# One layer's way from the output projection into its experts: projection in column parts, router logits read in place, rank and gather work reordered

## Chip, cores and metric

The kernel runs on one core of a Trainium2 chip. The metric is the device time in microseconds of one execution. All arithmetic is fp32. TensorE multiplies matrices into PSUM banks (eight, each 128 partitions by 512 columns), VectorE and ScalarE read and write banks and SBUF, SyncE issues nearly all DMA, GpSimd issues a few loads and the stores.

## What is computed

Two layers of a hybrid network over 288 tokens: 256 of a prompt and 32 of a running sample. A layer is (cut from the reference):

```python
merged = sigmoid(ga) * (a @ w_br_a) + sigmoid(gb) * (o @ w_br_b)       # attention and recurrence, 1024 wide
x = layernorm(DN_ALPHA * x + merged @ w_out, ln1_g, ln1_b)
moe_out = hier_moe(x, w_rg, w_re, w1, w3, w2)
ple_term = jax.nn.sigmoid(x @ w_ple_gate) * (ple @ w_ple)
x = layernorm(DN_ALPHA * x + moe_out + ple_term, ln2_g, ln2_b)

def hier_moe(...):                                                     # 4 groups of 8 experts, top 2 of the best group
    g_prob = softmax(xt @ w_rg);  g_top, g_idx = top_k(g_prob, 1)
    e_logits = (xt @ w_re).reshape(T, 4, 8)[the group g_idx]
    e_top, e_idx = top_k(softmax(e_logits), 2)
    wts = g_top * e_top / e_top.sum();  eidx = g_idx * 8 + e_idx
    return sum over the two experts of wts * ((silu(x @ w1[e]) * (x @ w3[e])) @ w2[e])
```

An expert has three matrices of 1024 x 512, 6.3 MB together, and there are 32 of them: 201 MB for each layer.

## The kernel before

The tokens are three tiles: 0 and 1 of 128 (the prompt), 2 of 32 (the sample). Each engine has one program, written out by hand, and runs it in order. `Book` numbers every TensorE job (a bank filled once) in the order of the lists `MIX_JOBS` and `expert_jobs`, which also give its bank. `job_done(eng, key)` waits until TensorE has finished that job, `emptied` and `job_read` are the signal and the wait for a bank that has been read, `open_bank` makes TensorE wait for the bank's last reader. `step` makes an engine wait for its own last instruction.

**The mix stage.** The output projection is the jobs `("wo", j, t)`: column half j of token tile t, each of two pieces of four 128-row chunks. Tiles go in the order 2, 0, 1 (`MIX_ORDER`). When a half is done, VectorE adds ALPHA * x and takes statistics (`mixed`), then normalises the tile (`normalize`). For tile 1 the normalisation is in two column halves, and the first one signals `x_half`, so that TensorE may transpose it early. TensorE turns the tile (`turn_mixed`, jobs `t1`), ScalarE and VectorE copy one half each into xT, and TensorE multiplies by the router weights `wr` (`router`, jobs `rt`, 36 columns: 4 group logits, 32 expert logits). VectorE then chooses the two experts of each token in a chain of small operations, each waiting for the one before (`route_tile`). It signals `route_out`.

**Rank and gather.** The experts are worked on in eight quads of four, and each expert has 32 places. `rank(t)` counts with small products, for each token, how many earlier tokens chose the same expert (jobs `rk`). `place_tile` turns that into a 0/1 matrix `sel` of tokens by places, and `gather_first` multiplies x by it, which collects the tokens of quad 0, transposed, in two banks (`XT0`, h = 0 and 1). ScalarE copies the first bank, VectorE the second, into `xeT`.

**Quads.** For each quad TensorE does G (gate projection), U (up projection), hT (transposes of silu(G) * U), Y (down projection) and C (combination of the rows into the tokens' sums); for the next quad it gathers the tokens (`gather`). A G, a U and a Y are each 64 TensorE instructions, in halves h = 0 and 1 over the rows of the weights. In quad 0, the transposes of the weighted choice (`ST0`) stand between G and U and wait for `selw_out`. VectorE makes that from the gate values (the loop at L2428 to L2434, then `weigh`), behind its copy of the second XT0 bank. The per-layer embedding term is the jobs `pl` and `pg` (`plain(j, t)` for column half j of tile t), and it is distributed over the program: (0, 2) while the mix stage routes tile 1, (0, 1) behind U of quad 0, (1, 2) behind its Y, and three more in quads 1 to 3 (`LATE_PLAIN`). `plain_gate` on ScalarE takes the sigmoid and `gated` on VectorE the product.

**Weights.** A piece of weights is 1 MiB (1,048,576 bytes) in an SBUF slot. SyncE issues the pieces of a layer in a fixed order, each when its slot has been read for the last time (`wait_used`). While the mix stage runs, 17 expert pieces find a slot. The next four have slots that G of quad 0 reads, and they come in two halves: `load_blocks` waits for `block_used`, which TensorE signals after two of the four chunks of G's first half, and then for `halves_used`, at the end of that half. Three further pieces wait for the end of that G. Then `load_unit` brings two pieces in one transfer of 2 MiB: six pieces (two units and two single pieces) when U of quad 0 is done, eight when Y of quad 0 is done, eight when G of quad 1 is done, and so on.

```python
if name == "G" and g == 0 and h == 0 and c == 1:
    ins.then_inc(block_used, 1)
```

All matrix products but the transposes are recorded at L1036 (`mm`), transposes at L1086, L1481 and L1570.

Of the kernel before, what the change touches and what calls it, by code (L numbers as in the profile page):

```python
# [180 lines left out]
def gated_tensor_jobs():  # L181
# [16 lines left out]
    for t in range(3):  # L198
        for j in range(len(PARTS[t])):
# [37 lines left out]
def expert_jobs(g):  # L237
# [16 lines left out]
    j += [(("Y", 0), 5), (("Y", 1), 6)] + (plain(1, 2, 1, 2) if g == 0 else []) + combine  # L254
# [52 lines left out]
def last_use(key):  # L307
# [14 lines left out]
    if name == "wo":  # L322
        return (name, key[1], 1)
# [100 lines left out]
def build(nc, x_prompt, x_sample, p_prompt, p_sample, cache_ckv, cache_krope, state_hgrn,  # L424
# [6 lines left out]
    with ctx:  # L431
# [28 lines left out]
        wr = sb("wr", 8 * 36)[:, :].rearrange("p (c n) -> p c n", c=8)  # L460
# [129 lines left out]
        mx = sm[:, 32:48]  # L590
        nb = sm[:, 48:64]
# [357 lines left out]
        def _(pool):  # L949
# [10 lines left out]
            for layer in range(DEPTH):  # L960
# [9 lines left out]
                pool.dma_start(wr[:, :, 0:4], w_router_group[layer].rearrange("(p c) n -> p c n", c=8)).then_inc(rows_in, 16)  # L970
                pool.dma_start(wr[:, :, 4:36], w_router_expert[layer].rearrange("(p c) n -> p c n", c=8)).then_inc(rows_in, 16)
# [49 lines left out]
        def _(pe):  # L1021
# [73 lines left out]
            for layer in range(DEPTH):  # L1095
# [256 lines left out]
                def router(t):  # L1352

                    b = open_bank((layer, "rt", t))
                    for c in range(8):
                        if c % 4 == 0:
                            job_read(pe, (layer, "t1", t, c // 4))
                        ins = mm(b[0:NT[t], 0:36], xT[:, c, T0[t]:T0[t] + NT[t]], wr[:, c, :], c == 0, c == 7)
                    done(ins)
# [36 lines left out]
                def rank(t):  # L1396

                    pe.wait_ge(route_out, 3 * layer + MIX_ORDER.index(t) + 1)
                    b = open_bank((layer, "rk", t))
                    for k, s in enumerate(MIX_ORDER[0:MIX_ORDER.index(t)]):  # L1400
                        mm(b[0:NT[t], 0:32], ones[0:NT[s], 0:NT[t]], route[0:NT[s], s, :], k == 0, False)
                    done(mm(b[0:NT[t], 0:32], tri[0:NT[t], 0:NT[t]], route[0:NT[t], t, :], t == MIX_ORDER[0], True))

                def gather_first(tiles):

                    for h in range(2):
                        key = (layer, "XT0", h)
                        b = open_bank(key) if tiles[0] == MIX_ORDER[0] else bank(key)
                        for t in tiles:
                            for c in range(4):  # L1410
                                k = 4 * h + c
                                ins = mm(b[:, c * P:(c + 1) * P], x[0:NT[t], t, k * P:k * P + P], sel[0:NT[t], t, :],
                                         t == MIX_ORDER[0] and c == 0, t == MIX_ORDER[2])
                        if tiles[-1] == MIX_ORDER[2]:
                            done(ins)
# [20 lines left out]
                gather_first((1,))  # L1436
# [91 lines left out]
                for g in range(QUADS):  # L1528
# [62 lines left out]
                    if g == 0:  # L1591
                        plain(1, 2)
# [28 lines left out]
        def _(act):  # L1621
# [40 lines left out]
            for layer in range(DEPTH):  # L1662
# [255 lines left out]
                plain_gate(0, 2)  # L1918

# [44 lines left out]
                for g in range(QUADS):  # L1964
# [19 lines left out]
                    if g == 0:  # L1984
                        plain_gate(1, 2)
# [26 lines left out]
        def _(dve):  # L2012
# [13 lines left out]
            def normalize(k, t, src, first_half=None, summed=None):  # L2026

                n, at = NT[t], ln_place(k, t)
                dve.bn_aggr(mvs[0:n, 2 * t:2 * t + 2], ln_st[0:n, :]).then_inc(ln_var, 1)
# [53 lines left out]
            for layer in range(DEPTH):  # L2083
# [255 lines left out]

                def route_tile(t):  # L2340
# [266 lines left out]
```

## Time and profile before

| | |
|---|---|
| median of 3 runs | 1529.52 us (1528.48 to 1530.48) |
| span of the profiled execution, first to last instruction | 1528.1 us |
| median less profiled span | 1.4 us |
| TensorE busy | 1285.5 us, 84% |
| VectorE busy | 403.9 us, 26% |
| ScalarE busy | 284.9 us, 19% |
| bytes moved by DMA | 488.78 MB, mean 320 GB/s |
| mean granted TensorE clock | 0.915 of 2.4 GHz |
| chain that ended last | TensorE 61%, DMA 34%, VectorE 3% |

A busy TensorE is not one at its peak, since its matmuls are pipelined and their ends are modelled. Times of single instructions are from this one execution, counted from its first instruction. The two layers follow one another with the same program: what layer 0 does at time t, layer 1 does some 750 us later.

### The profile page before, as it was taken

What the parts mean: (1) busy time and instruction counts of PE and PEld (TensorE: products, weight loads), DVE (VectorE), ACT (ScalarE), POOL (GpSimd) and SP (SyncE); (2) the same over time, 40 slices, a digit from 0 to 9 for tenths busy, and PEclk for the clock granted to TensorE, in tenths of its full rate; (3) what the DMA queues carried; (4) which work ended last, traced back from release to release, by engine and by line L of the source; (5) the groups of instructions that cost most, each with busy time, mean ns of one, the idle gap of its engine ahead of it and who ended that gap; (6) DMA issues with size and microseconds to landing.
All of it is one profiled execution on the core that took longest, in us unless ns stands there. A gap on an engine that the chain in (4) does not pass through costs nothing.

```text
span 1528.1 us, 20304 instructions
## 1 busy us (share of the span) xinstructions
PE 1285.5 (84%) x8528; PEld 723.5 (47%) x8529; DVE 403.9 (26%) x1027; ACT 284.9 (19%) x712; POOL 54.0 (4%) x94
## 2 busy tenths in 40 slices
PE   6999999999788767767799999999997886667655
PEld 4766887554332322322276678766442332223211
DVE  4142633542111101001133446245311111011003
ACT  2342522021001101000044434212111011010001
POOL 1300000000000000000022010000000000000000
PEclk9999999999898878788899999999998988788778
DMA  9503434999999999999972043579999999999994
GB/s 332 164 1 111 173 117 180 396 367 429 429 431 429 431 429 430 430 429 431 376 245 84 15 149 120 179 249 392 382 430 430 429 432 429 431 427 432 430 425 167
DMA packets 78799, 488.78 MB, mean 320 GB/s; under 512 B 7216, under 2 KB 13296, under 8 KB 49648
## 3 DMA queue, kind: packets, MB, share of 16 engines
q1 hardware_dynamic: 74240, 476.47, 75.9%
q0 software_dynamic: 4464, 10.93, 2.4%
q8 instruction: 73, 1.20, 0.3%
q14 instruction: 22, 0.18, 0.0%
HBM read 484.48 MB, written 2.89 MB: 319 GB/s over the span
## 4 chain that ended last, share of the span: by engine, by line
PE 61%; DMA 34%; DVE 3%; issue 1%; SPq 1%; ACT 0%; POOL 0%; DVEq 0%
PE bank L1036 59%; DMA ring<-in_w_e_down 12%; DMA ring<-in_w_e_up 9%; DMA ring<-in_w_e_gate 5%; DMA arena<-in_w_e_gate 4%; DMA arena<-in_w_e_up 4%; PE bank L1086 2%; DMA ring<-in_w_in 1%; DVE arena L2153 0%; SPq L933 0%; DVE arena L2041 0%; DVE x_sb L2050 0%; ACT xT L1642 0%; DVE small L2490 0%; DVE arena L2073 0%
## 5 line engine op out<-in xcount | busy, mean ns | idle before, releaser
L1036 PE MATMUL bank<-arena 128*32 128x512 f32 (+11 forms) x2808 | 572.3, 541 | 174.5 <-DMA ring<-in_w_e_up 71.0
L1036 PE MATMUL bank<-ring,arena 128*32 128x512 f32 (+4 forms) x1360 | 422.1, 650 | 32.3 <-DMA arena<-in_w_e_gate 15.7
L1036 PEld LDWEIGHTS bank<-arena 128*32 128x32 f32 (+6 forms) x2808 | 211.0, 137 | 441.1 <-issue 436.3
L1036 PE MATMUL bank<-ring,xT 128*32 128x128 f32 (+5 forms) x1536 | 237.5, 364 | 1.4 <-ACT xT L1642 1.1
L1036 PE MATMUL bank<-xT,ring 128*128 128x288 f32 x768 | 191.8, 407 | 0.0
L1036 PEld LDWEIGHTS bank<-ring,xT 128*32 128x32 f32 (+1 forms) x1536 | 121.6, 137 | 100.9 <-issue 90.5
L1036 PEld LDWEIGHTS bank<-ring,arena 128*32 128x32 f32 (+1 forms) x1360 | 108.5, 131 | 121.1 <-issue 114.4
L1036 PEld LDWEIGHTS bank<-xT,ring 128*128 128x128 f32 x768 | 143.7, 190 | 37.9
L1036 PE MATMUL bank<-arena,x_sb 128*128 128x128 f32 (+1 forms) x768 | 99.7, 282 | 1.4 <-DVE arena L2373 0.8
L1036 PEld LDWEIGHTS bank<-arena,x_sb 128*128 128x128 f32 (+1 forms) x768 | 90.5, 190 | 19.4 <-issue 12.7
L1036 PE MATMUL bank<-cst,arena 128*32 128x512 f32 x144 | 90.5, 788 | 0.0
L2546 DVE TENSOR_TENSOR arena<-arena,bank 128x512 f32<-128x512 f32 x16 | 11.0, 688 | 238.4 <-PE bank L1036 238.4
L1036 PE MATMUL bank<-arena,ring 128*128 128x288 f32 (+2 forms) x352 | 72.9, 372 | 0.0
L1036 PE MATMUL bank<-lb,arena 128*32 128x512 f32 x144 | 64.8, 592 | 0.0
L1036 PEld LDWEIGHTS bank<-arena,ring 128*128 128x128 f32 (+1 forms) x352 | 56.3, 180 | 14.8 <-issue 0.4
L2553 DVE COPY arena<-bank 128x512 f32<-128x512 f32 x16 | 11.1, 691 | 195.0 <-PE bank L1036 195.0
L1930 ACT COPY arena<-bank 128x512 f32<-128x512 f32 x16 | 9.4, 586 | 226.8 <-PE bank L1036 226.5
L2373 DVE TENSOR_TENSOR arena<-small,arena 128x128 f32<-128x128 f32 (+1 forms) x42 | 9.6, 283 | 151.2 <-PE bank L1036 151.2
L2483 DVE TENSOR_TENSOR arena<-arena,bank 128x512 f32<-128x512 f32 (+1 forms) x64 | 39.3, 629 | 23.2 <-PE bank L1036 23.2
L1983 ACT COPY arena<-bank 128x512 f32<-128x512 f32 x16 | 9.4, 586 | 173.9 <-PE bank L1036 173.9
L1967 ACT ACTIVATE arena<-bank 128x512 f32<-128x512 f32 x16 | 9.6, 597 | 161.4 <-PE bank L1036 161.4
L2419 DVE COPY arena<-bank 128x512 f32<-128x512 f32 x16 | 11.1, 691 | 80.3 <-PE bank L1036 80.3
(232 smaller groups left out, 877.7 us busy)
## 6 DMA issues: line engine op xcount, KB each, us to landing
arena<-in_w_e_up SPq DMA_DIRECT2D x34, 2048.0 KB, 32.1
arena<-in_w_e_gate SPq DMA_DIRECT2D x28, 2048.0 KB, 27.0
ring<-in_w_e_gate SPq DMA_DIRECT2D x24, 2048.0 KB, 25.1
ring<-in_w_e_up SPq DMA_DIRECT2D x20, 2048.0 KB, 24.7
arena<-in_w_e_down SPq DMA_DIRECT2D x20, 2048.0 KB, 22.4
ring<-in_w_e_down SPq DMA_DIRECT2D x18, 2048.0 KB, 25.2
ring<-in_w_in SPq DMA_DIRECT2D x32, 1024.0 KB, 9.4
arena<-in_w_e_gate SPq DMA_DIRECT2D x16, 1024.0 KB, 14.1
```

The costliest lines, as they stand in the source:

```text
L1036: return pe.matmul(out, lhsT, rhs, start=first, stop=last, skip_group_check=True)
L1086: ins = pe.transpose(b[0:m, a:a + src.shape[0]], src, ident[0:src.shape[0], 0:src.shape[0]])
L1930: emptied(act.copy(xeT[:, 0:4, :], bank(key)[:, :].rearrange("p (c t) -> p c t", c=4)), key)
L1967: emptied(act.activation(eh[:, :], bank(key)[:, :], ACT.Silu), key)
L1983: emptied(act.copy(ye[0], bank(key)[:, :]), key)
L2373: return dve.tensor_tensor(s4, bcast(places[0:n, :], 1, QUAD), bcast(ranks, 2, CAP), ALU.is_equal)
L2419: emptied(dve.tensor_copy(xeT[:, 4:8, :], bank(key)[:, :].rearrange("p (c t) -> p c t", c=4)), key)
L2483: emptied(dve.tensor_tensor(a, a, src, ALU.add), key)
L2546: emptied(dve.tensor_tensor(hid[:, :], eh[:, :], bank(key)[:, :], ALU.mult), key)
L2553: emptied(dve.tensor_copy(ye[1], bank(key)[:, :]), key)
```

## The change

Five edits, in both layers.

- The second column half of tile 1's output projection is computed as two jobs of 256 columns in two banks, and VectorE adds and takes statistics by quarters of the row (`mixed_in_parts`; the first half's job stays one).
- The group weights stand twice in `wr`, so the router has 40 columns. VectorE's `max` and `max_index` read the eight group columns from the bank, the copy to SBUF in front of them goes, and a copy for ScalarE is made after `route_out`.
- `rank` is split: `rank_earlier(t)` does the products over earlier tiles, `rank_own(t)` the tile's own. For tile 1 the first is moved ahead of `turn_mixed(1)`.
- `gather_first` takes the bank as an argument. Bank 0's part over tiles 2 and 0 stays ahead of `turn_mixed(1)`, bank 1's goes behind `router(1)`. Tile 1's part of bank 1 goes between the two halves of G of quad 0.
- `plain(0, 2)`, with its gate and product, moves from the routing of tile 1 to behind Y of quad 0.

```diff
 MIX_JOBS = [...
-            (("rk", 2), 4), (("rk", 0), 5), (("wo", 1, 1), 2), (("t1", 1, 0), 0), (("t1", 1, 1), 1), (("rt", 1), 3),
-            (("pl", 0, 2), 2), (("pg", 0, 2), 5), (("rk", 1), 4), (("XT0", 0), 6), (("XT0", 1), 7), (("cnt",), 3)]
+            (("rk", 2), 4), (("rk", 0), 5), (("wo", 1, 1, 0), 2), (("wo", 1, 1, 1), 1), (("t1", 1, 0), 0), (("t1", 1, 1), 5), (("rt", 1), 3),
+            (("rk", 1), 4), (("XT0", 0), 6), (("cnt",), 3), (("XT0", 1), 7)]
...
-    j += [(("Y", 0), 5), (("Y", 1), 6)] + (plain(1, 2, 1, 2) if g == 0 else []) + combine
+    j += [(("Y", 0), 5), (("Y", 1), 6)] + (plain(0, 2, 3, 4) + plain(1, 2, 1, 2) if g == 0 else []) + combine
...
-                pool.dma_start(wr[:, :, 0:4], w_router_group[layer].rearrange("(p c) n -> p c n", c=8)).then_inc(rows_in, 16)
-                pool.dma_start(wr[:, :, 4:36], w_router_expert[layer].rearrange("(p c) n -> p c n", c=8)).then_inc(rows_in, 16)
+                pool.dma_start(wr[:, :, 0:8], w_router_group[layer].rearrange("(p c) n -> p c n", c=8)).then_inc(rows_in, 16)
+                pool.dma_start(wr[:, :, 8:40], w_router_expert[layer].rearrange("(p c) n -> p c n", c=8)).then_inc(rows_in, 16)
...
+                def last_mix(h):
+                    n = piece_number(layer, ("wo", 1, h))
+                    arrived(n)
+                    w = slot(n).rearrange("p (c n) -> p c n", c=4)
+                    for part in range(2):
+                        key = (layer, "wo", 1, 1, part)
+                        b = open_bank(key) if h == 0 else bank(key)
+                        for c in range(4):
+                            ins = mm(b[:, 0:256], mT[:, 4 * h + c, T0[1]:T0[1] + P], w[:, c, 256 * part:256 * part + 256], h + c == 0, h + c == 4)
+                        if h == 1:
+                            done(ins)
...
                 router(0)
-                half_mix(1, 0)
-                rank(2)
-                rank(0)
-                half_mix(1, 1)
+                last_mix(0)
+                for t in (2, 0):
+                    rank_earlier(t)
+                    rank_own(t)
+                last_mix(1)
                 pe.wait_ge(sel_early, layer + 1)
-                gather_first((2, 0))
+                gather_first((2, 0), 0)
+                rank_earlier(1)
                 turn_mixed(1)
                 router(1)
+                gather_first((2, 0), 1)
                 pe.wait_ge(ple_in, 32 * (layer + 1))
-                plain(0, 2)
-                rank(1)
+                rank_own(1)
                 pe.wait_ge(sel_out, QUADS * layer + 1)
-                gather_first((1,))
+                gather_first((1,), 0)
                 b = open_bank((layer, "cnt"))
...
                         for h in range(2):
+                            if name == "G" and g == 0 and h == 1:
+                                gather_first((1,), 1)
                             if name == "G":
...
                     if g == 0:
+                        plain(0, 2)
                         plain(1, 2)
...
+                def mixed_in_parts(j):
+                    for part in range(2):
+                        at = 2 * j + part
+                        xt = x[:, 1, 256 * at:256 * at + 256]
...
+                        ins = dve.scalar_tensor_tensor(xt, xt, ALPHA, src, ALU.mult, ALU.add)
...
+                        ins = dve.bn_stats(stats_quarters[:, 6 * at:6 * at + 6], xt)
+                    step(ins)
...
-                    step(dve.tensor_copy(lg[:, 0:4], b[0:n, 0:4]))
-                    step(dve.max(r[:, 0:8], lg[:, 0:8]))
-                    step(dve.max_index(ri[:, 8:16], r[:, 0:8], lg[:, 0:8]))
+                    step(dve.max(r[:, 0:8], b[0:n, 0:8]))
+                    step(dve.max_index(ri[:, 8:16], r[:, 0:8], b[0:n, 0:8]))
...
                     dve.scalar_tensor_tensor(route[0:n, t, :], iota[0:n, :], r[:, 41:42], oh[:, 0:32],
                                              ALU.is_equal, ALU.add).then_inc(route_out, 1)
+                    emptied(dve.tensor_copy(lg[:, 0:4], b[0:n, 0:4]), key)
...
-                gated(0, 2)
                 for g in range(QUADS):
...
                     if g == 0:
+                        gated(0, 2)
                         gated(1, 2)
```

On ScalarE `plain_gate(0, 2)` moves in the same way, from ahead of the copy of XT0's first bank to behind the copy of Y in quad 0. On the host the group weights are written twice side by side.

## Rows read from the trace of the kernel before

**Rows 1.** Chain that ended last, in order of time: start us, length us, what.
```profile
370.44 10.41 DMA ring<-in_w_e_up
...
380.98 7.11 PE bank L1036 x64
...
1120.35 11.43 DMA ring<-in_w_e_up
...
1131.91 8.80 PE bank L1036 x64
```

**Rows 2.** Windows of 1 us in layer 0: length, busy by engine, clock, DMA share, GB/s.
```profile
317.00:318.00 1.00, 1.00 (x12) 0.88 (x12) 0.00 (x0) 0.86 (x3) 0.00 (x0) 1.00 0.27 115
...
321.00:322.00 1.00, 1.00 (x16) 0.28 (x11) 0.83 (x6) 0.00 (x0) 0.00 (x0) 1.00 1.00 143
322.00:323.00 1.00, 1.00 (x12) 0.26 (x8) 0.83 (x5) 0.00 (x0) 0.00 (x0) 1.00 0.61 168
323.00:324.00 1.00, 1.00 (x16) 0.37 (x12) 0.93 (x6) 0.00 (x0) 0.00 (x0) 1.00 1.03 397
```

**Rows 3.** Timeline of SyncE's DMA issues: start us, length us, what.
```profile
320.27 4.36 SPq L860 DMA_DIRECT2D arena<-in_w_e_down  x8
```

**Rows 4.** Timeline of TensorE, layer 0: start us, length us, what, idle before.
```profile
300.73 3.68 PE L1036 MATMUL bank<-ring,xT 128*128 128x512 f32 x8
304.34 4.41 PE L1036 MATMUL bank<-arena,x_sb 32*128 32x128 f32 x32
308.59 1.13 PE L1086 MATMUL bank<-cst,x_sb 128*128 128x128 f32 x8
309.96 1.95 PE L1036 MATMUL bank<-wr,xT 128*128 128x36 f32 x16 [0.24 <-ACT xT L1642]
311.84 0.64 PE L1036 MATMUL bank<-ring,arena 128*32 128x128 f32 x16
312.30 1.93 PE L1036 MATMUL bank<-ring,xT 128*32 128x128 f32 x64
314.61 0.96 PE L1036 MATMUL bank<-arena,cst 32*128 32x32 f32 x6 [0.38 <-DVE arena L2363]
315.95 2.05 PE L1036 MATMUL bank<-arena,x_sb 128*128 128x128 f32 x16 [0.38 <-DVE arena L2373]
...
318.28 7.07 PE L1036 MATMUL bank<-arena 128*32 128x512 f32 x64
```

**Rows 5.** Timeline of VectorE, layer 0.
```profile
304.45 0.69 DVE L2335 SCALAR_TENSOR_TENSOR x_sb<-x_sb,bank 128x512 f32<-128x512 f32 x1 [3.13 <-PE bank L1036]
...
307.60 1.41 DVE L2050 SCALAR_TENSOR_TENSOR x_sb<-x_sb,small,lnw 128x512 f32<-128x512 f32 x2
...
311.94 0.16 DVE L2350 COPY arena<-bank 128x4 f32<-128x4 f32 x1 [1.49 <-PE bank L1036]
...
318.04 0.69 DVE L2419 COPY arena<-bank 128x512 f32<-128x512 f32 x1 [2.04 <-PE bank L1036]
...
323.05 0.68 DVE L2414 TENSOR_TENSOR arena<-arena 128x128 f32<-128x128 f32 x3
...
356.39 0.42 DVE L2483 TENSOR_TENSOR arena<-arena,bank 128x256 f32<-128x256 f32 x1
```

**Rows 6.** Timeline of ScalarE, layer 0.
```profile
317.15 0.59 ACT L1930 COPY arena<-bank 128x512 f32<-128x512 f32 x1
```

**Rows 7.** DMA packets from 319 to 370.44 us, and from 1069 to 1120.35 us.
```profile
DMA packets 2629, 20.55 MB, mean 399 GB/s; under 512 B 286, under 2 KB 286, under 8 KB 1310
...
DMA packets 2587, 20.01 MB, mean 390 GB/s; under 512 B 277, under 2 KB 277, under 8 KB 1301
```

**Rows 8.** Window of 10 us in layer 1, columns as in rows 2.
```profile
1130.00:1140.00 10.00, 8.09 (x60) 2.84 (x64) 2.23 (x3) 0.00 (x0) 0.00 (x0) 0.83 1.00 428
```

**Rows 9.** Timeline of TensorE at quad 1's U, first rows, layer 0 and 1.
```profile
380.98 0.63 PE L1036 MATMUL bank<-arena 128*32 128x512 f32 x3 [1.87 <-DMA ring<-in_w_e_up]
...
1131.91 0.71 PE L1036 MATMUL bank<-arena 128*32 128x512 f32 x3 [2.89 <-DMA ring<-in_w_e_up]
```

More of the change, by code:

```diff
@@ L1399, in rank, with rank_earlier, rank_own @@
+                def rank_earlier(t):
                     b = open_bank((layer, "rk", t))
                     for k, s in enumerate(MIX_ORDER[0:MIX_ORDER.index(t)]):
+                        pe.wait_ge(route_out, 3 * layer + k + 1)
                         mm(b[0:NT[t], 0:32], ones[0:NT[s], 0:NT[t]], route[0:NT[s], s, :], k == 0, False)
+                def rank_own(t):
+                    pe.wait_ge(route_out, 3 * layer + MIX_ORDER.index(t) + 1)
+                    b = bank((layer, "rk", t))
@@ L1402, in rank, with gather_first @@
                     done(mm(b[0:NT[t], 0:32], tri[0:NT[t], 0:NT[t]], route[0:NT[t], t, :], t == MIX_ORDER[0], True))
[L1404 to L1415, printed above, removed]
+                def gather_first(tiles, h):
+                    key = (layer, "XT0", h)
+                    b = open_bank(key) if tiles[0] == MIX_ORDER[0] else bank(key)
+                    for t in tiles:
+                        for c in range(4):
+                            k = 4 * h + c
+                            ins = mm(b[:, c * P:(c + 1) * P], x[0:NT[t], t, k * P:k * P + P], sel[0:NT[t], t, :],
+                                     t == MIX_ORDER[0] and c == 0, t == MIX_ORDER[2])
+                    if tiles[-1] == MIX_ORDER[2]:
+                        done(ins)
@@ L2338, in mixed @@
                     step(half_stats(t, x[:, t, :], j))
+                def mixed_in_parts(j):
+                    for part in range(2):
+                        at = 2 * j + part
+                        xt = x[:, 1, 256 * at:256 * at + 256]
+                        if j == 0:
+                            src = bank((layer, "wo", 0, 1))[:, 256 * part:256 * part + 256]
+                            if part == 0:
+                                job_done(dve, (layer, "wo", 0, 1))
+                        else:
+                            job_done(dve, (layer, "wo", 1, 1, part))
+                            src = bank((layer, "wo", 1, 1, part))[:, 0:256]
+                        ins = dve.scalar_tensor_tensor(xt, xt, ALPHA, src, ALU.mult, ALU.add)
+                        if j == 1:
+                            emptied(ins, (layer, "wo", 1, 1, part))
+                            job_read(dve, (layer, "wo", 1, 1, part))
+                        elif part == 1:
+                            emptied(ins, (layer, "wo", 0, 1))
+                            job_read(dve, (layer, "wo", 0, 1))
+                        else:
+                            step(ins)
+                        ins = dve.bn_stats(stats_quarters[:, 6 * at:6 * at + 6], xt)
+                    step(ins)
                 def route_tile(t):
@@ L2395, in _ @@
                 place_tile(0).then_inc(sel_early, 1)
-                mixed(1, 1)
-                normalize(1 + 2 * layer, 1, x[:, 1, :], x_half)
+                mixed_in_parts(1)
+                normalize(1 + 2 * layer, 1, x[:, 1, :], x_half, stats=stats_quarters)
                 read_x("t1", layer, xT, (1,))
```

26 lines of the change are left out of this document (12 added, 14 removed).

## Prediction

> **What bounds the kernel now.** I read the page first, then the chain of work that ended last, then the stretch that the change touches on TensorE, VectorE and ScalarE, then the weight stream, and last quad 0 and 1 of the experts. The chain tells which resource sets the end. From about 370 us in layer 0, and from 1120 us in layer 1, it steps between a weight transfer and the 64 TensorE instructions that release the next slot; the first pair of each layer are [rows 1]. The DMA engines are full there, and a layer's 201 MB of expert weights is what the time is made of. So an edit counts only if it moves the stream.
>
> The stream has one hole per layer. At 317 us the engines move 115 GB/s, having finished all that had a free slot, and at 321 still only 143 [rows 2]. SyncE issues the next pieces at 320.27 [rows 3], because load_blocks waits for block_used, which TensorE signals when a quarter of quad 0's G is done. Whatever starts G earlier shortens the hole. G's 64 instructions start at 318.28 [rows 4]. Layer 1 repeats all this 749.9 us later (its issue after G of quad 1 at 1120.35, layer 0's at 370.44 [rows 1]).
>
> The path to G is a relay [rows 4 to 6]: VectorE adds and normalises tile 1; TensorE, at 308.59, transposes it; ScalarE and VectorE copy; TensorE's router (309.96, 1.95 us); VectorE's route chain (from 311.94); TensorE's rank (314.61, six instructions, 0.96 us); one VectorE compare; 16 gather instructions (from 315.95, 2.05 us) and the count; G. TensorE's plain(0, 2), 311.84 to 314.23, lies under the route chain.
>
> **The change up to G, layer 0.** 1. The last projection: eight instructions of 512 columns (3.68 us [rows 4]) become sixteen of 256, the same columns; I take no change, since a router instruction, which also loads a 128-column weight, takes 1.95/16 = 0.12 us, under the 0.23 us of 256 columns. The bounds are 0 and +0.4 us. On VectorE the last add and statistics, two of 0.69 us, cover only half the columns: a 128x256 form takes 0.42 [rows 5], so 2 x (0.69 - 0.42) = 0.54 us less. The aggregate then reads four records, for at most some 0.1 more. I take -0.5.
> 2. Transposes of tile 1. Now x_half is signalled at 307.60 + 0.71 = 308.3 us, but TensorE was in a gather of 32 instructions (4.41 us) until 308.59. Afterwards it does 16 of them (to 306.6) and four rank instructions (4/6 of 0.96, to 307.2), and waits for x_half at 307.8. The transposes start at 307.85: -0.75. The router, a few columns wider, ends 0.75 earlier.
> 3. The route chain loses its first copy (0.16 us [rows 5], with its wait an estimated 0.19); max and max_index read the bank instead, for 0 to 0.1 us more. -0.15; rank may start at 313.7 where it was 314.61.
> 4. TensorE does 16 gather instructions (2.2 us) meanwhile, to 313.35, so these take plain(0, 2)'s cover. Then rank_own is two instructions for six: 0.35 for 0.96, -0.6. The tile's choice is ready 0.75 + 0.15 + 0.6 = 1.5 us earlier, and the gather starts at 314.45.
> 5. Before G: 16 instructions and the count took 2.33 us (315.95 to 318.28). Now eight instructions (1.03), 0.1 us of signals and ScalarE's copy (0.59 [rows 6]), to 316.2; the count fits beside the copy, and the sigmoid's table load has gone from before it. G starts **2.1 us earlier**, and the stream resumes 2.1 us earlier.
> Cost at nothing: the wider router rows (two loads long ahead), the VectorE split of part 0, which ends at 296.65 as the router does, and the removed memsets. The SyncE queue is past them. If the cover of part 0 is gone, 0.1 us moves route_out of tile 0, which TensorE reads 0.7 us later.
>
> **What it costs behind G.** 6. The second half of G now stands behind eight gather instructions (1.03 us) and VectorE's copy of the second half (0.69) with 0.1 of signals: +1.83. G ends at 325.35 - 2.1 + 1.8 = 325.1.
> 7. VectorE is an in-order queue: behind that copy stand the weights of the three tiles. From the copy's start (318.04) to the last product (323.05 + 0.68) it is 5.7 us [rows 5]. The copy now starts at 316.2 + 3.5 + 1.03 + 0.05 = 320.8, so the products end at 326.5, and TensorE's transposes ahead of U, which wait for them, start then and not right behind G, as now at 325.3. U starts **1.2 us later** than now, after two TensorE stalls of 0.8 and 1.4 us.
> 8. plain(0, 2), 311.84 to 314.23 [rows 4], 2.4 us, now stands between Y and the combines. TensorE runs on there without a wait of note, so nothing hides it: G of quad 1 ends 1.2 + 2.4 = **3.6 us later**. Its vector and scalar work (0.3 us each) lies under it.
> 9. SyncE waits for that end with the next four units: 374.0 for 370.44, 1123.95 for 1120.35. Is the queue still full? From the restart to 370.44 SyncE had issued 21 pieces of 1,048,576 bytes (four in halves, three, six, eight): 22.02 MB. Moved were 20.55 in layer 0 and 20.01 in layer 1 [rows 7]: 1.47 and 2.01 MB left, at the 0.428 MB/us of [rows 8] 3.4 and 4.7 us of work. With the stream 2.1 us early these run out at 371.75 and 1122.95. A restart from empty has a lag too. Its lower bound is 0.7 us: 320.27 to the first bytes behind 321.0. Its upper bound is 2.1: up to 324.0 the engines moved 143 + 168 + 397 KB, 1.65 us of work in 3.73. I take 1.0, near the lower end, as here each issue is 2 MB and there half of one. The new holes are 2.25 + 1.0 = 3.2 and 1.0 + 1.0 = 2.0 us.
> The same reckoning at the issue behind Y of quad 0 (1.2 us late) leaves some cover in both layers, and I charge nothing there; if that cover is gone, it is another few tenths.
> From there transfers set the pace again: quad 1's U, after plain of quad 1, starts at most 1.7 us late, into a queue that holds over 5 us.
>
> **The sum.** Layer 0: -2.1 + 3.2 = +1.1 us. Layer 1: -2.1 + 2.0 = -0.1. Span 1528.1 + 1.0 = 1529.1. The median of the runs is 1529.52, 1.4 over the profiled span, so the forecast is **1530.5 us**. The hole before quad 0 shrinks and a new one opens behind quad 1's G. With the lag at 0.7 and 2.1 it is 1529.9 and 1532.7.
>
> The restart is where the skill speaks against this change. The trace has 0.7 to 2.1 us for it [rows 2, 3]. The Trainium skill (DMA: Bandwidth & Descriptors, Anatomy of one DMA) puts a fixed cost of about 2.0 us on each transfer, by a fit made for transfers that GpSimd issues. An estimate from that page makes the holes 4.2 and 3.0 us and the time 1532.5; the row's nearer end gives 1529.9.
>
> **Rivals.** *The whole gain stays*: the queue never runs dry behind quad 1's G, as its cover (3.4 and 4.7 us) must then exceed the relative delay of 2.1 + 3.6. It would if the weights chain or plain(0, 2) cost TensorE much less than reckoned. For it: nothing in the trace shows the two stalls of steps 6 and 7, which are put together from rows. Against: both are in-order work on the engine that SyncE waits for. Time: 1529.5 - 4.2 = 1525.3. Chance 0.2.
> *G starts only 1 us earlier*, because the column split gives nothing (the 256-column pieces cost TensorE 0.4 us, and reads from the bank are slow). Every later TensorE event is then 1.1 us later than above, and it is they that set the new hole: +2.2 us, 1532.7, slower. For it: steps 1 and 3 rest on forms that the trace doesn't have. It decides from 1.0 us of lost gain per layer. Chance 0.12.
> *The clock falls in quad 0.* In layer 1 TensorE idled 2.89 us before quad 1's U [rows 9], and the granted clock of the stretch from 1130 us is 0.83 [rows 8], with the 64 instructions at 8.80 us, a mix of the two levels of 2.4 and 1.2 GHz. After an idle 1.87 us in layer 0 they took 7.11 [rows 1, 9]. The new stalls are 0.8 and 1.4 us, apart by 3.5 us of work. If they count together, U takes 1.7 us more per layer: +3.4, 1533.9, slower. Chance 0.08. The Trainium skill (TensorE: Matmul & The Clock Gate, HAM oscillation) has the same pattern, short bursts between waits for data that halve the clock; by it as by the rows, two stalls this short should not do it.
>
> **How the numbers follow.** My forecast holds 0.6. The measurement can tell about 0.2%, 3.1 us. Faster is the first rival, 0.2; within 0.2% the forecast, 0.6; slower the last two, 0.2. The range runs from the first rival, 1525.0, to between the second and the third, 1533.6, and leaves out the third and the far side of the first.
>
> **What the profile will show.** Right: G of quad 0 near 316.2 (316 to 316.5), two short TensorE stalls around it, the transposes ahead of U near 326.5, SyncE's issue after quad 1's G near 374, and bytes near zero just before it, in both layers but shorter in layer 1. Wrong: no hole at 372 us, with all of layer 1 over 2 us early; or G no earlier than 317; or a granted clock under 1.0 before 370. Most exposed is step 9, a difference of two sums: 1 us of error in the cover moves the result by 1 us per layer.

## The result, and the profile after

The changed kernel takes 1542.13 us (median of 4 runs, 1538.35 to 1543.3), the kernel before on the same chip 1529.69. The ratio is 1.008, with a 95% interval of 1.0068 to 1.0092: 12.4 us slower, outside the forecast's range. The profiled execution is the fastest of the four, with a span of 1536.2 us and 1538.35 in all. It shows 8.1 us of span more than before's; the rest is runs that had no profile.

TensorE's timeline of the changed kernel, layer 0 (start us, length us, what, idle before), answers to [rows 4]:

```profile
306.19 0.74 PE L1037 MATMUL bank<-arena,cst 32*128 32x32 f32 x4
307.60 1.32 PE L1087 MATMUL bank<-cst,x_sb 128*128 128x128 f32 x8 [0.67 <-DVE x_sb L2072]
309.02 1.95 PE L1037 MATMUL bank<-wr,xT 128*128 128x40 f32 x16
310.90 2.75 PE L1037 MATMUL bank<-arena,x_sb 32*128 32x128 f32 x16
313.58 0.61 PE L1037 MATMUL bank<-arena,cst 128*128 128x32 f32 x2
314.56 2.08 PE L1037 MATMUL bank<-arena,x_sb 128*128 128x128 f32 x8 [0.38 <-DVE arena L2418]
...
317.36 4.57 PE L1037 MATMUL bank<-arena 128*32 128x512 f32 x32 [0.23 <-issue]
321.86 1.16 PE L1037 MATMUL bank<-arena,x_sb 128*128 128x128 f32 x8
323.80 3.64 PE L1037 MATMUL bank<-arena 128*32 128x512 f32 x32 [0.78 <-DVE arena L2463]
328.81 0.61 PE L1501 MATMUL bank<-cst,arena 128*128 128x128 f32 x3 [1.36 <-DVE arena L2458]
```

Up to the router all is as forecast (transposes at 307.60, router at 309.02). Then the same kind of work takes longer. Eight gather instructions take 2.08 us at 314.56 and 1.16 at 321.86; the first half of G takes 4.57 us and the second half 3.64. G starts at 317.36, only 0.9 us earlier than before. The windows of the changed kernel say why (last three columns: granted clock, DMA share, GB/s), and answer to [rows 2]:

```profile
311.00:312.00 1.00, 1.00 (x9) 0.88 (x9) 0.85 (x6) 0.00 (x0) 0.00 (x0) 1.00 1.03 426
312.00:313.00 1.00, 1.00 (x7) 1.00 (x7) 0.86 (x6) 0.00 (x0) 0.00 (x0) 0.73 1.05 418
313.00:314.00 1.00, 1.00 (x6) 0.81 (x4) 0.73 (x6) 0.20 (x1) 0.00 (x0) 0.50 1.01 410
...
318.00:319.00 1.00, 1.00 (x8) 0.22 (x4) 0.00 (x0) 0.56 (x1) 0.00 (x0) 0.50 0.04 16
319.00:320.00 1.00, 1.00 (x12) 0.36 (x8) 0.00 (x0) 0.00 (x0) 0.00 (x0) 0.86 0.00 0
```

The granted clock is 0.50, TensorE's lower level of 1.2 GHz, from the middle of the window at 312 until after 319. Before the change it was 1.00 there (the column before the last two in [rows 2]). SyncE's timeline, changed kernel:

```profile
320.27 4.01 SPq L861 DMA_DIRECT2D arena<-in_w_e_down  x8
...
376.14 0.33 SPq L934 DMA_DIRECT2D ring<-in_w_e_up  x1
```

The stream restarts at 320.27, the very moment of [rows 3], so nothing is gained: `block_used` comes after a quarter of G, and that quarter began at 1.2 GHz. From G's start to the issue it is 2.9 us, where it was 2.0. The issue behind quad 1's G comes at 376.14, 5.7 us later than the 370.44 of [rows 1]: the forecast's 3.6 and the 2.1 that were not gained. The second hole is there, and wider for it (windows, changed kernel):

```profile
374.00:375.00 1.00, 1.00 (x14) 0.27 (x9) 0.00 (x0) 0.00 (x0) 0.00 (x0) 1.00 0.77 328
375.00:376.00 1.00, 1.00 (x13) 0.16 (x5) 0.00 (x0) 0.00 (x0) 0.00 (x0) 1.00 0.16 66
376.00:377.00 1.00, 1.00 (x7) 0.52 (x4) 0.86 (x4) 0.88 (x2) 0.00 (x0) 1.00 0.04 16
377.00:378.00 1.00, 1.00 (x4) 0.50 (x3) 0.50 (x3) 1.00 (x1) 0.00 (x0) 1.00 1.22 262
```

Two of the forecast's own signs of being wrong are there: G of quad 0 no earlier than 317, and a granted clock under 1.0 before 370.

VectorE did as forecast. Its timeline, changed kernel, answers to [rows 5]: the adds of a quarter row take 0.42 us, the aggregate of 24 numbers 0.26, max from the bank 0.17.

```profile
304.13 0.42 DVE L2374 SCALAR_TENSOR_TENSOR x_sb<-x_sb,bank 128x256 f32<-128x256 f32 x1 [0.84 <-PE bank L1037]
...
305.05 0.26 DVE L2051 BATCH_NORM_AGGREGATE small<-small 128x2 f32<-128x24 f32 x1
...
311.01 0.17 DVE L2396 MAX8 arena<-bank 128x8 f32<-128x8 f32 x1 [1.36 <-PE bank L1037]
```

### The profile page after: what moved, and what is told of

Its sections match the earlier page's. It is cut to its first block, busy times and chain, and to the rows that moved or that the text cites. A ratio compares the mean times of both kernels' runs of the same rounds, so it can differ in the third digit from the quotient of the medians.

```text
span 1536.2 us, 20370 instructions
## 1 busy us (share of the span) xinstructions
PE 1283.4 (84%) x8560; PEld 732.0 (48%) x8561; DVE 404.8 (26%) x1029; ACT 282.3 (18%) x710; POOL 54.0 (4%) x94
## 4 chain that ended last, share of the span: by engine, by line
PE 58%; DMA 34%; DVE 3%; SPq 3%; issue 1%; ACT 0%; POOL 0%; DVEq 0%
PE bank L1037 56%; DMA ring<-in_w_e_down 5%; DMA ring<-in_w_e_gate 5%; DMA ring<-in_w_e_up 5%; DMA arena<-in_w_e_up 4%; DMA arena<-in_w_e_gate 4%; DMA cst<-in_w_e_down 4%; DMA cst<-in_w_e_gate 3%; DMA arena<-in_w_e_down 2%; PE bank L1087 2%; SPq L873 2%; DMA ring<-in_w_in 1%; SPq L934 0%; DVE arena L2175 0%; DVE x_sb L2072 0%
## 5 line engine op out<-in xcount | busy, mean ns | idle before, releaser
L1037 PE MATMUL bank<-arena 128*32 128x512 f32 (+11 forms) x2808 | 564.3, 534 | 177.9 <-DMA ring<-in_w_e_up 67.7
L1037 PE MATMUL bank<-ring,arena 128*32 128x512 f32 (+4 forms) x1360 | 412.0, 640 | 36.4 <-DMA arena<-in_w_e_gate 19.8
L1037 PE MATMUL bank<-ring,xT 128*32 128x128 f32 (+6 forms) x1568 | 237.4, 360 | 1.3 <-ACT xT L1665 1.1
L1037 PEld LDWEIGHTS bank<-ring,xT 128*32 128x32 f32 (+1 forms) x1568 | 127.6, 138 | 96.4 <-issue 84.6
L1037 PE MATMUL bank<-arena,x_sb 128*128 128x128 f32 (+1 forms) x768 | 103.6, 288 | 1.4 <-DVE arena L2418 0.8
L1037 PE MATMUL bank<-cst,arena 128*32 128x512 f32 x144 | 86.5, 758 | 0.0
```

The costliest lines, as they stand in the source:

```text
L1037: return pe.matmul(out, lhsT, rhs, start=first, stop=last, skip_group_check=True)
```

## Experiments

Each kernel was timed beside the kernel before on the same chip. "So many us over before" is the difference of the two medians of one chip. Kernels of different sets are compared by what each has over its own reference. The ratio and its 95% interval are taken over all runs; the ratio can differ from that of the two medians by up to 0.0007.

**First set: what holds the clock, and what the late steps cost.** `plain_alone` is one part of the change alone, in the kernel before:

```diff
                 router(1)
                 pe.wait_ge(ple_in, 32 * (layer + 1))
-                plain(0, 2)
                 rank(1)
...
                     if g == 0:
+                        plain(0, 2)
                         plain(1, 2)
```

(and its gate and product likewise). Expected:

> The kernel before with one edit: plain(0, 2), its gate and its product moved from the routing of tile 1 to behind Y of quad 0. Theory A (the product under the route chain kept TensorE's clock at 2.4 GHz, and without it the clock falls to 1.2 just ahead of quad 0): the granted clock is 0.5 for some us between 312 and 320, quad 0's G starts later than the 318.28 of before, the stream restarts 1 to 2 us later, G of quad 1 ends 3.5 to 5 us later (374 to 375.5), and a hole opens behind it: 4 to 9 us slower than before. Theory B (clock is no matter, only the 2.4 us of TensorE work between Y and the combines): the clock stays 1.00 until 370, the stream restarts at 320.3 as before, G of quad 1 ends 2.4 us later, which the 3.4 us of queued transfers cover or nearly so: 0 to 2 us slower.

Measured: 1535.57 us against 1529.66, ratio 1.0043 (1.0026 to 1.0059): 5.9 slower. TensorE's timeline of plain_alone:

```profile
309.88 1.95 PE L1036 MATMUL bank<-wr,xT 128*128 128x36 f32 x16 [0.24 <-ACT xT L1642]
314.57 1.59 PE L1036 MATMUL bank<-arena,cst 32*128 32x32 f32 x6 [2.75 <-issue]
316.55 3.55 PE L1036 MATMUL bank<-arena,x_sb 128*128 128x128 f32 x16 [0.38 <-DVE arena L2372]
...
320.38 7.07 PE L1036 MATMUL bank<-arena 128*32 128x512 f32 x64
```

TensorE idles 2.75 us behind the router, and the rank then takes 1.59 us where it took 0.96, the gather 3.55 where it took 2.05 [rows 4]; the clock is 0.50 in the window from 314 to 316. G starts 2.1 us late. This is theory A. How much of the 5.9 us is the clock's, and how much the 2.4 us of work now behind Y, this run alone can't tell; `plain_alone_filled` below bears on it.

`plain_back` undoes that part in the changed kernel; `plain(0, 2)` stands between `gather_first((2, 0), 1)` and `rank_own(1)`.

```diff
                 gather_first((2, 0), 1)
                 pe.wait_ge(ple_in, 32 * (layer + 1))
+                plain(0, 2)
                 rank_own(1)
...
                     if g == 0:
-                        plain(0, 2)
                         plain(1, 2)
```

> The changed kernel with plain(0, 2), its gate and product put back, between the gather of tiles 2 and 0 and rank_own(1). Theory A (clock): the clock stays 1.00 to 370 us; rank is about 2 us behind route_out (TensorE has 4.6 us of work there), so G of quad 0 starts near 318.2, as before the change; G of quad 1 ends about 3.2 us later than before, not 5.7; 0 to 3 us slower than before, so 9 to 12 faster than the changed kernel. Theory B (the changes inside G and the waits for the weights of the tiles make the loss): G of quad 1 ends 3 us late all the same, and the time stays 5 us or more above before.

Measured: 1542.76 against 1529.66, ratio 1.0091 (1.0074 to 1.0108), as slow as the changed kernel. The expectation from theory A missed. From two windows and TensorE's timeline of plain_back:

```profile
310.00:312.00 2.00, 2.00 (x15) 1.83 (x15) 1.20 (x8) 0.00 (x0) 0.00 (x0) 0.92 1.04 426
312.00:314.00 2.00, 2.00 (x20) 1.74 (x22) 1.25 (x9) 0.60 (x4) 0.00 (x0) 0.50 1.00 406
```

```profile
313.48 1.08 PE L1037 MATMUL bank<-ring,arena 128*32 128x128 f32 x16
```

The clock fell all the same, before `plain(0, 2)` began at 313.48; on top this work kept rank waiting, and G started only at 319.24. So having this product somewhere under the route chain is not enough in the changed kernel. Whether it would have held the clock right behind the router, its place before the change, was not tested.

`filler` adds work to the changed kernel that computes nothing:

```diff
                 rank_earlier(1)
+                mm(open_bank((layer, "t1", 1, 0))[:, :], ones, cst[:, 0:512], True, True)
                 turn_mixed(1)
                 router(1)
+                mm(open_bank((layer, "XT0", 1))[:, :], ones, cst[:, 0:512], True, True)
                 gather_first((2, 0), 1)
```

> The changed kernel with two products of 128x512 added whose results are thrown away (four TensorE instructions, 0.92 us each pair): one where TensorE waits for x_half, one ahead of the gather behind router(1). Nothing is left out. Theory A (clock): the added work holds the clock at 1.00; G of quad 0 starts near 317.3 and the stream restarts near 319.3, one us ahead of before, although TensorE has 1.8 us more to do; quad 1's G ends 2 us sooner than in the changed kernel: 3 to 8 us faster than it. Theory B (clock no matter): the added work costs its own time, G starts up to 1 us later than in the changed kernel, and the time is the same or 1 to 2 us worse.

Measured: 1535.87 against 1529.66, ratio 1.0042 (1.0025 to 1.0059): 6.2 over before where the changed kernel has 12.4, so 6.2 faster with two more products of 1.10 us per layer for TensorE to do. TensorE's timeline and then two windows of filler:

```profile
314.35 1.16 PE L1037 MATMUL bank<-arena,x_sb 128*128 128x128 f32 x8 [0.38 <-DVE arena L2420]
...
316.23 3.64 PE L1037 MATMUL bank<-arena 128*32 128x512 f32 x32 [0.37 <-issue]
```

```profile
312.00:314.00 2.00, 1.97 (x17) 1.73 (x15) 1.37 (x10) 0.46 (x3) 0.00 (x0) 1.00 1.01 406
316.00:318.00 2.00, 1.77 (x20) 0.71 (x24) 0.00 (x0) 1.41 (x2) 0.00 (x0) 1.00 0.31 131
```

The clock stays 1.00, the eight gather instructions are back at 1.16 us, and G starts at 316.23, where the forecast has 316.2. The stream restarts at 318.20, and the issue behind quad 1's G comes at 374.07, forecast 374.0. With the clock held, the forecast's times for G, the restart and this issue are met, and yet the kernel is 6.2 us slower than before, where the forecast says 1.0.

`weights_first` puts VectorE's chain for the weights of the tiles ahead of its copy.

```diff
                 place_tile(1).then_inc(sel_out, 1)
...
-                read_tokens((layer, "XT0", 1))
                 for t in range(3):
...
                 weigh(slice(0, QUAD)).then_inc(selw_out, 1)
+                read_tokens((layer, "XT0", 1))
```

> The changed kernel with VectorE's weights of the three tiles (the loop of seven small operations per tile, then the product) put ahead of its copy of the second XT0 bank. Theory A and my steps 6 and 7: the weights are made under the first half of G, TensorE no longer waits 1.4 us ahead of the transposes of the choice, so U of quad 0 and all behind it come 1.4 us sooner; G of quad 1 ends near 374.7 and not 376.1; 2.5 to 3 us faster than the changed kernel (1.4 per layer), still 7 to 10 slower than before. If the copy is then late itself (the chain takes 5.1 us from 315, to 320.1, and the bank is ready at 321.8 or later), it isn't. Rival: the loss is all in the clock and in plain(0, 2), and VectorE's order gives under 1 us.

Measured: 1541.13 against 1529.66, ratio 1.008 (1.0063 to 1.0097), 11.5 over before. Layer 0 did as expected (issue behind quad 1's G at 374.03 for 376.14), but the clock was low for longer in layer 1 of the profiled run (granted 0.50 in the windows from 1063 to 1076 us; the changed kernel has 0.50 from 1067 to 1073). The gain of 1.0 us is not clear of the intervals. It is repeated below with the clock held.

**Second set: the 5 us that the forecast does not have.** I compared how many bytes had been moved at equal times. In the stretches where the stream alone sets the pace, the changed kernel and three of these four fell behind steadily (plain_alone did not). DMA packets from 480 to 700 us, kernel before:

```profile
DMA packets 7069, 94.55 MB, mean 430 GB/s; under 512 B 786, under 2 KB 786, under 8 KB 786
```

and in filler:

```profile
DMA packets 7041, 94.19 MB, mean 428 GB/s; under 512 B 780, under 2 KB 780, under 8 KB 780
```

plain_alone, whose router isn't widened, has 94.57 MB. The wide router makes `wr` 128 bytes longer, and all that is placed behind it moves by as much, the arena with its ten slots among it. In the kernel before, the first arena slot begins at byte 146688 of each partition, 573 times 256; now it begins at 146816. The eight slots of the ring stand ahead of `wr` and don't move; they begin 128 bytes off a multiple of 256 (byte 4224) in every kernel here. `pad_only` is the kernel before with that alone:

```diff
-        wr = sb("wr", 8 * 36)[:, :].rearrange("p (c n) -> p c n", c=8)
+        wr = sb("wr", 8 * 40)[:, 0:8 * 36].rearrange("p (c n) -> p c n", c=8)
```

> The kernel before with one edit: the router's weights get room for 8 x 40 columns in SBUF and still hold 8 x 36, so every tensor that is placed behind them, the ten arena slots of expert weights among them, begins 128 bytes further on; no instruction changes. In the last four kernels the three with the wide router fell behind steadily in the stretch where transfers alone set the pace (1.9 us from 80 to 240 MB of layer 0), and the one without it, plain_alone, by 0.3. Theory A (place in SBUF): an arena slot now begins 128 bytes off a multiple of 256, where before it was on one, each write into it is a little dearer, and the kernel is 3 to 4.5 us slower than before, with the whole loss spread over the expert stretches and none at quad 0. The Trainium skill (DMA: Bandwidth & Descriptors, How a descriptor splits into AXI transactions) has such a rule, by which a descriptor that does not start at a multiple of 256 bytes takes one transaction more. Theory B (the drift comes from the order of the work): no difference, within 1 us of before.

Measured: 1532.99 against 1529.2, ratio 1.003 (1.0018 to 1.0041), 3.8 slower with no instruction added, removed or moved. DMA packets of pad_only from 480 to 700 us:

```profile
DMA packets 7042, 94.14 MB, mean 428 GB/s; under 512 B 784, under 2 KB 784, under 8 KB 784
```

`filler_aligned` takes the shift out of filler:

```diff
-        sm = sb("small", 192)
+        sm = sb("small", 160)
```

> Kernel filler with one edit: the tensor of small columns is 160 wide and not 192 (the last 32 are unused), which puts all that lies behind it at the very place it has in the kernel before. Theory A (place in SBUF): 3 to 4.5 us faster than filler's 1535.9, so 1531.5 to 1533, and no steady drift against before between 80 and 240 MB. Theory B: 1535 to 1537 as filler.

Measured: 1532.23 against 1529.2, ratio 1.0026 (1.0016 to 1.0036): 3.0 over before where filler has 6.2, so 3.2 faster. The same stretch, filler_aligned:

```profile
DMA packets 7066, 94.60 MB, mean 430 GB/s; under 512 B 780, under 2 KB 780, under 8 KB 780
```

What is left, 3.0 us (2.4 to 5.5 by the interval), is what the forecast puts at 1.0. Windows of filler_aligned around the two late issues of each layer:

```profile
350.00:358.00 8.00, 8.00 (x182) 5.71 (x175) 2.24 (x5) 1.14 (x3) 0.00 (x0) 1.00 0.97 381
370.00:380.00 10.00, 10.00 (x54) 3.75 (x47) 1.37 (x6) 1.88 (x2) 0.00 (x0) 1.00 0.80 310
1100.00:1110.00 10.00, 10.00 (x204) 6.26 (x197) 1.53 (x4) 1.14 (x3) 0.00 (x0) 1.00 0.95 376
1120.00:1130.00 10.00, 10.00 (x72) 3.45 (x65) 1.37 (x6) 3.36 (x4) 0.00 (x0) 1.00 0.82 316
```

Before, the same windows have 433, 431, 434 and 433 GB/s. The lost time is 8 x (1 - 381/433) = 1.0, then 2.8, 1.3 and 2.7 us. Behind Y the queue was not empty: the engines move 434 GB/s in the window at 351, in which SyncE issues, and only then less (SyncE's timeline and two windows of filler_aligned). In layer 1 the issue is at 1104.28, with 426 GB/s in the window at 1103 and 360, 262 and 221 behind it.

```profile
351.50 0.33 SPq L934 DMA_DIRECT2D arena<-in_w_e_gate  x1
```

```profile
352.00:353.00 1.00, 1.00 (x48) 1.00 (x40) 0.22 (x1) 0.00 (x0) 0.00 (x0) 1.00 1.00 295
353.00:354.00 1.00, 1.00 (x48) 1.00 (x40) 0.00 (x0) 0.28 (x1) 0.00 (x0) 1.00 0.77 270
```

`weights_first_clocked` is filler_aligned with the edit of weights_first.

> Kernel filler_aligned with VectorE's weights of the three tiles put ahead of its copy of the second XT0 bank, so step 7 without the clock in the way. Theory A: quad 1's G ends 1.4 to 2 us sooner than in filler_aligned, the hole behind it shrinks by as much, and the time falls by 2.5 to 4 us, to 1528 to 1530. Rival: the hole behind quad 1's G does not depend on when it ends, and the time stays.

Measured: 1529.29 against 1529.2, ratio 1.0002 (0.9993 to 1.0011), 2.9 faster than filler_aligned. Its transposes ahead of U (TensorE's timeline) wait for nothing any more:

```profile
326.53 0.61 PE L1503 MATMUL bank<-cst,arena 128*128 128x128 f32 x3
```

`gather_whole` is filler_aligned with tile 1's part of the second bank ahead of G again:

```diff
                 gather_first((1,), 0)
+                gather_first((1,), 1)
...
-                            if name == "G" and g == 0 and h == 1:
-                                gather_first((1,), 1)
```

> Kernel filler_aligned with the gather of tile 1 into the second bank put back ahead of G of quad 0, as before the change. G starts 0.7 to 1.0 us later (317.2), the stream restarts near 319.1, but G is no longer interrupted (1.8 us) and the weights are ready in time (1.4 us): U of quad 0 starts at 324.8, a good us ahead of before, and G of quad 1 ends near 371.3 with plain(0, 2) still behind Y. Theory A: the queued transfers cover that, so no new hole; 1 us per layer gained at the restart; 1527 to 1529, faster than before by 0.5 to 2.5 us. Rival (any work added between Y and the combines opens the hole behind quad 1's G): 1530 or more.

Measured: 1526.94 against 1529.2, ratio 0.9987 (0.9978 to 0.9996), 2.3 faster than before and the fastest of all. SyncE's timeline, and windows, of gather_whole:

```profile
320.04 4.02 SPq L861 DMA_DIRECT2D arena<-in_w_e_down  x8
...
372.39 0.33 SPq L934 DMA_DIRECT2D ring<-in_w_e_up  x1
```

```profile
370.00:380.00 10.00, 10.00 (x42) 4.01 (x35) 1.37 (x6) 1.88 (x2) 0.00 (x0) 1.00 1.00 411
...
1120.00:1130.00 10.00, 10.00 (x42) 3.96 (x35) 1.37 (x6) 1.88 (x2) 0.00 (x0) 1.00 0.99 408
```

This profiled execution, 1530.04 us, is the slowest of eleven, and it runs late by 1 to 1.5 us from early in layer 0 (its transposes of tile 1 start at 308.78, filler_aligned's at 307.42). Between the restart and the issue behind quad 1's G it takes 52.35 us, filler_aligned 55.87, and before 50.17 [rows 1, 3]. The holes at 370 and 1120 have shrunk to 0.5 and 0.6 us.

**Third set: the clock again.** `after_aligned` is the changed kernel with the edit of filler_aligned.

> The changed kernel with one edit: the tensor of small columns 160 wide and not 192, so that the arena lies where it lies before the change. If placement and clock add up, this takes off pad_only's 3.5 to 3.8 us and no more: 1538 to 1539, with the clock still at 0.50 from 312 to 319 us; filler_aligned at 1532.2 is then the same kernel with the clock held, and the clock's price is 6 us. If they don't add up (the steady drift matters less when the stream has more holes): 1540 or more.

Measured: 1540.29 against 1528.78, ratio 1.0069 (1.0056 to 1.0082). That is 11.5 over before where the changed kernel had 12.4, less of a gain than pad_only's 3.8, and the median lies in the other branch of the expectation, 1540 or more. The interval reaches down to 1537.3 and takes in both branches, so this run does not decide whether place and clock add up. The profiled run shows one thing in which these kernels scatter. Its clock fell earlier and stayed low for about twice as long; from TensorE's timeline and two windows of after_aligned:

```profile
309.61 3.03 PE L1037 MATMUL bank<-wr,xT 128*128 128x40 f32 x16
312.57 4.08 PE L1037 MATMUL bank<-arena,x_sb 32*128 32x128 f32 x16
```

```profile
310.00:312.00 2.00, 2.00 (x12) 2.00 (x12) 0.23 (x1) 0.40 (x3) 0.00 (x0) 0.56 0.98 410
322.00:324.00 2.00, 2.00 (x15) 0.45 (x8) 0.00 (x0) 0.00 (x0) 0.00 (x0) 0.53 0.00 0
```

G is at 320.09 there, and in layer 1 it was low for the shorter time.

`plain_alone_filled` is plain_alone with two of the added products behind the router:

```diff
                 router(1)
+                for _ in range(2):
+                    mm(open_bank((layer, "rk", 1))[:, :], ones, cst[:, 0:512], True, True)
```

> Kernel plain_alone with two products of 128x512 added whose results are thrown away, behind router(1), where TensorE idles for 2.75 us. Nothing is left out. Clock theory: the clock stays 1.00, quad 0's G starts at 318.3 as before the change and the stream restarts at 320.3; what stays is the 2.4 us behind Y, with a hole of about 1 us per layer behind quad 1's G: 1530 to 1532, so 4 to 6 us faster than plain_alone's 1535.6. Rival (idle time itself and the late G): no change from 1535.6.

Measured: 1531.76 against 1528.78, ratio 1.0016 (1.0007 to 1.0025), 3.0 over its reference where plain_alone has 5.9 over its own. In the profiled run the clock held to 315 us, and in layer 1's routing throughout, but fell to 0.50 in layer 0 in the window from 316 to 318. The added work helps, and it isn't always enough.

`whole_first_only` and `whole_second_only` leave out one of gather_whole's two added products each.

> Kernel gather_whole without its second added product (the one behind router(1)); the one in the wait for x_half stays. If that one alone holds the clock: G starts 0.9 us earlier, 317.2, and the time is 1525 to 1526.5, the fastest so far. If the clock falls as in the changed kernel, from 312 us on: 1529 to 1534, with G at 318 or later. The clock fell after a stretch of narrow products (32 rows or 32 to 128 columns), so I expect the fall, 6 to 4.

> Kernel gather_whole without its first added product (in the wait for x_half); the one behind router(1) stays. If the idle 0.67 us before the transposes is what lets the clock fall, it falls here: 1529 to 1534. If wide work at 311 us is enough to hold it: 1526 to 1527, a few tenths under gather_whole's 1526.9, as the transposes start 0.2 us sooner. I expect it to hold, 6 to 4, as plain(0, 2) stood in the same place.

Measured: 1529.85 (ratio 1.0005, 0.9996 to 1.0014) and 1534.5 (ratio 1.0044, 1.0027 to 1.0061), both against 1528.78: 1.1 and 5.7 over before, where gather_whole is 2.3 under. In both profiled runs the clock fell in layer 0, to 0.73 and 0.55 in the window from 310 to 312. In layer 1 it fell in whole_first_only and held in whole_second_only. With the product behind the router alone I had expected it to hold, and it did not. From TensorE's timeline and a window of whole_second_only:

```profile
309.41 2.88 PE L1037 MATMUL bank<-wr,xT 128*128 128x40 f32 x16
312.10 2.06 PE L1037 MATMUL bank<-cst 128*128 128x512 f32 x2
```

```profile
310.00:312.00 2.00, 2.00 (x13) 2.00 (x12) 0.04 (x1) 0.20 (x2) 0.00 (x0) 0.55 1.00 418
```

The clock fell while the router ran, before the added product behind it could start at 312.10. In such an execution nothing that stands behind the router can prevent the fall. Either product by itself is not enough in the runs seen; both together held the clock in all four profiles taken with both (filler, filler_aligned, weights_first_clocked, gather_whole).

## Why the prediction was wrong

**The step that failed first is step 4 with step 5**, "these take plain(0, 2)'s cover" and "G starts 2.1 us earlier". I priced `plain(0, 2)` as 2.4 us of work that hides under the route chain, and its successor, a gather of 16 narrow instructions, at the full clock. Without it the stretch from 304 to 314 us is narrow products and a wait of 0.67 us, and the clock goes to 1.2 GHz. Shown by plain_alone (that edit alone: clock 0.50, 5.9 slower) and by filler (clock held by useless work: 6.2 faster than the changed kernel, G at 316.23). It is shown that the gather, the rank and the start of G ran at 1.2 GHz, and that this took the gain at the restart. Which edit let the clock fall in the changed kernel is not. Moving `plain(0, 2)` is enough in the kernel before, but in plain_back, with the product back in a later place, the clock fell too, and in after_aligned and whole_second_only it fell while the router still ran. Up to there these kernels differ from the one before by steps 1 and 2, above all by 16 gather instructions ahead of the transposes and not 32, and a wait of 0.67 us. I had the clock as a rival, but at the stalls inside quad 0, with a chance of 0.08. It fell ahead of them, and there, in the windows at 323 and 328, it stayed 1.00. The Trainium skill (TensorE: Matmul & The Clock Gate, HAM oscillation) describes the fall by waits for data; in the changed kernel no wait in front of it was over 0.67 us in layer 0, so that form of the rule did not warn of it.

**"Cost at nothing: the wider router rows" failed.** 128 bytes of SBUF moved the arena slots off a multiple of 256 bytes. I had asked what the wider rows cost to load and to multiply, and not what is placed behind them. It is 3.8 us by pad_only and 3.2 by filler against filler_aligned. The Trainium skill (DMA: Bandwidth & Descriptors, How a descriptor splits into AXI transactions) names a mechanism: a descriptor that starts off such a multiple begins with a transaction from the boundary below it, which makes one more for a length such as 576 bytes. It says this of reads, and these are writes. The runs show that the place costs 0.4% of the stream's rate (94.55 to 94.14 MB in 220 us), and not that this is why; no place but these two was tried.

**Step 9 was right in kind and too small.** The hole behind quad 1's G exists, and its issue came at 374.07 in filler as reckoned. But the holes are 2.8 and 2.7 us, where I had 3.2 and 2.0, and the issue behind Y, which I charged nothing, costs 1.0 and 1.3. That is 7.8 us for 5.2. Two restarts that each gain 2.1 us leave 3.7 of it, and the medians say 3.0, where the forecast has 1.0. The largest term that I had wrong is the one put at nothing: I counted a lag only where the queue is empty, and behind Y the rate fell to 270 and 221 GB/s with the queue still moving. The lag itself was taken too small as well: in the changed kernel the issue is at 376.14 and by 378 the engines had moved at most 16 + 262 KB, 0.65 us of work in 1.86, and by 379 another 295 KB, 1.34 us in 2.86, a lag of 1.5 us at least, where I took 1.0. And some of the rate is lost ahead of the issue (328 and 66 GB/s at 374 and 375).

**Right:** steps 1 to 3 (transposes at 307.60 for 307.85, max from the bank at no price); step 6 (the second half of G waits 0.78 us); step 7 (the transposes ahead of U wait 1.36 us for VectorE, forecast 1.4), with weights_first_clocked showing that it costs 2.9 us in all; step 8 (2.2 us: the two plain products start at 353.26 and 355.44 in the changed kernel).

**The sum.** The 12.4 us over before are 6.2 for the clock (filler), 3.2 for the place of the arena (filler_aligned), and 3.0 for the holes behind quad 0 less the gain at the restart. These shares are not exact: the intervals of the runs are 1.5 to 2.6 us to each side, and after_aligned, which removes the place first, gives place and clock as 0.9 and 8.5. The clock's share may also be larger than filler shows, since the added products can cost time of their own.

What stays open: whether the narrow products, the short wait or both let the clock fall, as filler changes both; why it fell at 310 us in some profiles and at 312 in others, and stayed low once or twice as long. The unprofiled runs of the changed kernel, 3 to 5 us over the profiled one, would fit the longer form, but no profile of them was taken.

## What to carry to other kernels

Work that hides under another engine's chain may also be what keeps TensorE at its full clock; before moving it, look at how narrow the work around it is and how long the engine waits there, and read the granted clock in small windows afterwards, since the whole run's mean (0.915 before, 0.914 after) shows nothing. When a tensor grows, check where everything allocated behind it now begins. Here the ring's eight slots begin 128 bytes off a multiple of 256 in every kernel, and what moving them would give was not tried. A transfer queue's cover is the difference of two large sums, so moving work from ahead of a release to behind it should be priced at every release until the queue is deep again.

## What the runs showed of the hardware

- TensorE's clock can fall from 2.4 to 1.2 GHz with no wait over 0.67 us in front of it and while the engine is working: in the changed kernel it was busy 0.93, 0.40, 0.91 and 0.98 of the windows from 306 to 309 us and fully from 310 on, with narrow products, and the clock fell in the window at 312. It was back in the window at 319, during the wide products of G. Two idle times of 0.78 and 1.36 us shortly after, around the second half of G, left it at 1.00.
- With the ten arena slots beginning 128 bytes off a multiple of 256, the weight stream ran at 428 GB/s and not 430, in five kernels of five (94.14 to 94.23 MB from 480 to 700 us: the changed kernel, plain_back, filler, weights_first, pad_only), and at 430 in the nine that had the old place (94.55 to 94.65 MB, the kernel before among them).
- After an issue into a queue that was running out, the rate dipped even where the queue had not been empty: 434 GB/s in the window of the issue, then 295 and 270 in the next two (filler_aligned, issue at 351.50 us).
